# The second head's turned shares copied by ScalarE instead of VectorE, in a fused two-model kernel

## What is computed

```
p = softmax(mask(q @ k.T * scale + bias))     # 128 queries at a time, keys 0..(i+1)*128
out = p @ v
```

## Time and profile before

| | |
|---|---|
| median of 3 runs | 2183.3 us (2180.8 to 2186.79) |
| the profiled execution's own time | 2181.09 us |
| its span, first to last instruction | 2179.3 us |
| mean granted TensorE clock | 0.986 |
| busy: TensorE matmuls | 2073.2 us (95%) |
| busy: VectorE, ScalarE, GpSimd | 45%, 42%, 40% |

### The profile page before, as it was taken

The page is one execution under the profiler, slowest core; times in us unless marked ns, Lnnn a source line. Parts: engine busy times, 40 slices in busy tenths (PEclk is TensorE's granted clock), DMA queues, the critical chain, the costliest instruction groups (busy, mean ns, idle before and its releaser), DMA issues. The chain is left out here.

```text
span 2179.3 us, 28917 instructions
## 1 busy us (share of the span) xinstructions
PE 2073.2 (95%) x10248; PEld 1652.2 (76%) x10248; DVE 986.0 (45%) x1312; ACT 910.2 (42%) x1773; POOL 874.4 (40%) x648
## 2 busy tenths in 40 slices
PE   7999999999999978899999998989999999999997
PEld 5887688888887756688888886766667878888885
DVE  6454545312255677542312265666554544323134
ACT  4555443323343654442323355655554333223233
POOL 3232254444454221254444453542113545445454
PEclk9999999999999999999999999999999999999998
DMA  4212122222222110122222221221101222222222
GB/s 142 68 68 78 39 97 97 97 97 96 97 97 87 58 39 20 39 97 97 97 97 96 96 97 66 89 87 40 39 30 58 97 84 91 99 95 97 100 94 104
DMA packets 50613, 177.96 MB, mean 82 GB/s; under 512 B 5568, under 2 KB 5832, under 8 KB 50512
## 3 DMA queue, kind: packets, MB, share of 16 engines
q1 hardware_dynamic: 47536, 171.08, 22.6%
q10 hardware_dynamic: 2976, 5.48, 0.7%
HBM read 174.43 MB, written 2.12 MB: 81 GB/s over the span
## 5 line engine op out<-in xcount | busy, mean ns | idle before, releaser
L424 POOL TENSOR_TENSOR w_lo<-raw,w_hi 128x512 fp32r<-128x512 f32 x644 | 874.2, 1379 | 1285.1 <-ACT w_hi L1021 1285.1
L1021 ACT ACTIVATE w_hi<-raw 128x512 fp32r<-128x512 f32 x644 | 371.0, 624 | 849.1 <-PE gemm_banks L451 828.8
L449 PE MATMUL gemm_banks<-h_hi,w_hi 128*128 128x512 f32 x1512 | 613.7, 406 | 8.0 <-POOL w_lo L424 2.8
L451 PE MATMUL gemm_banks<-h_hi,w_lo 128*128 128x512 f32 x1512 | 592.7, 392 | 0.0
L450 PE MATMUL gemm_banks<-h_lo,w_hi 128*128 128x512 f32 x1512 | 592.1, 392 | 0.0
L449 PEld LDWEIGHTS gemm_banks<-h_hi,w_hi 128*128 128x128 f32 x1512 | 284.6, 188 | 92.4 <-issue 24.2
L449 PE MATMUL gemm_banks<-u_hi,w_hi 128*128 128x512 f32 x848 | 330.3, 390 | 4.2 <-POOL w_lo L424 2.9
L451 PEld LDWEIGHTS gemm_banks<-h_hi,w_lo 128*128 128x128 f32 x1512 | 284.2, 188 | 62.7
L450 PE MATMUL gemm_banks<-u_lo,w_hi 128*128 128x512 f32 x848 | 329.9, 389 | 0.0
L451 PE MATMUL gemm_banks<-u_hi,w_lo 128*128 128x512 f32 x848 | 329.9, 389 | 0.0
L450 PEld LDWEIGHTS gemm_banks<-h_lo,w_hi 128*128 128x128 f32 x1512 | 285.0, 188 | 56.6 <-issue 2.4
(11 more groups left out here) (308 smaller groups left out, 1980.2 us busy)
## 6 DMA issues: line engine op xcount, KB each, us to landing
raw<-slabs SPq DMA_DIRECT2D x322, 512.0 KB, 3.2
t_raw<-rel_rows ACTq DMA_DIRECT2D x4, 512.0 KB, 3.8
y_t<-x ACTq DMA_DIRECT2D x8, 256.0 KB, 2.1
x<-x_t SPq DMA_DIRECT2D x4, 256.0 KB, 6.7
x<-x_t ACTq DMA_DIRECT2D x4, 256.0 KB, 6.9
consts<-consts_packed SPq DMA_DIRECT2D x1, 516.5 KB, 8.7
cos<-pos SPq DMA_DIRECT2D x2, 256.0 KB, 10.1
params<-params_packed ACTq DMA_DIRECT2D x1, 211.5 KB, 4.3
```

The costliest lines, as they stand in the source:

```text
L424: pool.tensor_tensor(w_lo[:, j, part], raw[:, j, part], w_hi[:, j, part].bitcast(F32), ALU.subtract).then_inc(slab_split, 1)
L449: pe.matmul(out, high, rhs_hi, start=first, stop=False)
L451: return pe.matmul(out, low, rhs_hi, start=False, stop=last)
L1021: act.activation(w_hi[:, m % 2, part], raw[:, m % 2, part], ACT.Copy).then_inc(slab_hi, 1)
```

## The change

In the 80 steps that turn two heads' softmax shares (32 of the first block, 16 of the second, 32 of the third), VectorE's copy takes the first head alone, and a new ScalarE activation, `take_second`, copies the second head's. It stands in ScalarE's stream behind `weigh(s)` and the products' first half and ahead of `even(s)`. TensorE waits for both copies, by a second semaphore, ahead of every `bias_of` and `values`.

```
+            def take_second(n, w, need):
+                act.wait_ge(flipped, n + 1)
+                if need:
+                    act.wait_ge(valued, need)
+                act.activation(turned[:, 1, 0:w], SC[:, 2 * (n % 2) + 1, 0:w], ACT.Copy).then_inc(taken_b, 1)
...
                 if s < AB_STEPS:
                     weigh(s, (s % 4 + 1) * P)
                 products(*half(s, 0))
+                if s >= 1:
+                    take_second(s - 1, ((s - 1) % 4 + 1) * P, 2 * (s - 1))
                 if s < AB_STEPS:
                     even(s, (s % 4 + 1) * P, s + 1)
...
                 if s >= 2:
                     pe.wait_ge(taken, s - 1)
+                    pe.wait_ge(taken_b, second_takes(s - 1))
...
-                dve.tensor_copy(turned[:, :, 0:w], SC[:, 2 * b:2 * b + 2, 0:w]).then_inc(taken, 1)
+                dve.tensor_copy(turned[:, 0, 0:w], SC[:, 2 * b, 0:w]).then_inc(taken, 1)
```

More of the change, by code:

```diff
@@ L257, in e_valued, with second_takes @@
     return 128 + (s if s <= DIFF_STEPS else 2 * s - DIFF_STEPS)
+def second_takes(n):
+    first = AB_STEPS + STICK_STEPS
+    return min(n, AB_STEPS) + min(max(n - first, 0), CD_STEPS - STICK_STEPS) + max(n - E_BASE - DIFF_STEPS, 0)
 def build(nc, slabs, x_in, params_in, consts_in, pos1_in, pos2_in, rel_in, lam_in, y_out):
@@ L385, in build @@
         shared, evened, flipped = sem("shared"), sem("evened"), sem("flipped")
-        taken, valued = sem("taken"), sem("valued")
+        taken, taken_b, valued = sem("taken"), sem("taken_b"), sem("valued")
         qk_hi, qk_split = sem("qk_hi"), sem("qk_split")
@@ L576, in values @@
                 pe.wait_ge(taken, s + 1)
+                pe.wait_ge(taken_b, second_takes(s + 1))
                 if i == 0:
@@ L713, in cd_bias @@
                     pe.wait_ge(taken, AB_STEPS + s - 1)
+                    pe.wait_ge(taken_b, second_takes(AB_STEPS + s - 1))
                 mask = strict_r if p < 4 else chunk_r
@@ L752, in cd_values @@
                 pe.wait_ge(taken, AB_STEPS + s + 1)
+                pe.wait_ge(taken_b, second_takes(AB_STEPS + s + 1))
                 if i == 0:
@@ L895, in e_bias @@
                     pe.wait_ge(taken, E_BASE + s - 1)
+                    pe.wait_ge(taken_b, second_takes(E_BASE + s - 1))
                 for head in range(2):
@@ L936, in e_values @@
                 pe.wait_ge(taken, E_BASE + s + 1)
+                pe.wait_ge(taken_b, second_takes(E_BASE + s + 1))
                 if br == 0:
@@ L1306, in _ @@
                 cd_products(*cd_half(s, 0))
+                if s > STICK_STEPS:
+                    take_second(AB_STEPS + s - 1, ((s - 1) % 4 + 1) * P, 64 + 2 * (s - 1))
                 if STICK_STEPS <= s < CD_STEPS:
@@ L1411, in _ @@
                 e_half(2 * s)
+                if s > DIFF_STEPS:
+                    take_second(E_BASE + s - 1, e_step(s - 1)[3], e_valued(s - 1))
                 if s < DIFF_STEPS:
@@ L1847, in cd_take @@
                     dve.wait_ge(valued, 64 + 2 * s)
-                dve.tensor_copy(turned[:, :, 0:w], SC[:, 2 * b:2 * b + 2, 0:w]).then_inc(taken, 1)
+                if s < STICK_STEPS:
+                    last = dve.tensor_copy(turned[:, :, 0:w], SC[:, 2 * b:2 * b + 2, 0:w])
+                else:
+                    last = dve.tensor_copy(turned[:, 0, 0:w], SC[:, 2 * b, 0:w])
+                last.then_inc(taken, 1)
             def cd_shares(s):
```

## The result

The changed kernel takes 2189.2 us (median of 12 runs, 2186.62 to 2190.85), the kernel before 2183.6 us on the same chip (12 runs, 2180.8 to 2186.79). The ratio is 1.0023, 95% interval 1.0014 to 1.0032: about 5 us slower. That is slower beyond doubt, and inside the 0.3% that the prediction set as its limit of "no change". The profiled execution took 2189.12 us, span 2187.3, granted clock 0.984 (the mean share of 2.4 GHz that TensorE was given; its other level is 1.2 GHz). The prediction said 2193 us, with 2186 to 2201 as its range.

The account below looks back on a forecast made before the run. TensorE, its matmuls filling 95% of the span, was taken as the bound. Blocks of +0.9, +3.9 and +3.7 us make +8.6; with 1.2 for clock, 2181.1 becomes 2190.9, and 2.2 to the median gives 2193, range 2186 to 2201.

Parts of the forecast that it names:

- The bound and the order: TensorE's waits for the copy matter; ScalarE's in-order stream, with its copy behind both Exps, decides each of 80 steps.
- Price of the copy: ScalarE's copy out of PSUM was put at 0.27, 0.37, 0.48 and 0.58 us for the four widths.
- late and early steps: Late: Exps delay ScalarE's copy, +0.39 to +0.61 us in the first block; early: ScalarE is free, -7.0 us in 17 steps.
- TensorE's 0.05 us after a copy: Time TensorE needs between a copy's end and the next bias, read from a VectorE copy and used for ScalarE's.
- the sum: The three blocks' changes in waits, less what is absorbed: +0.9, +3.9 and +3.7, in all +8.6 us.
- What is absorbed: Delays given back: in the second block -1.7 at stalls and 0.86 at a full VectorE queue; 2.3 us behind the swap.
- the stalls: Second block: three times a +0.57 us delay precedes TensorE's 2.4 us stall for VectorE's rotated query, giving back 1.7 us.
- the swap: Third block: ScalarE's copy behind the swap delays the bias +3.9 us; 2.3 us come back, leaving +1.6.
- The clock: Added TensorE idling of 7.6 us would lower the granted clock: 2.5 us, of which half, 1.2 us, was charged.
- Hidden after all: Rival, 25 in 100: late copies delay only TensorE and work in hand absorbs half the sum, +4 us, 2187.
- Faster: Rival, 6 in 100: ScalarE's Exps are over when the flips end, so waits shrink by 13.2 us everywhere, 2170.
- Much slower: Rival, 9 in 100: nothing absorbed, copies 0.1 us dearer in 30 late steps, full clock loss: about +20 us, 2204.

Follow-up runs that it names:

- late_only: Against the kernel before, ScalarE copies the second head only in the 31 steps where its copy comes late; VectorE copies both elsewhere: 2197.17 us, ratio 1.0063.
- early_only: Against the kernel before, ScalarE copies the second head only in the 17 steps whose Exps end before the flips do: 2172.56 us, ratio 0.9944.
- e_only: Against the kernel before, ScalarE copies the second head only in the third block's 32 two-head steps: 2188.36 us, ratio 1.0019.
- copy_twice: Against the changed kernel, ScalarE makes each second copy twice before telling TensorE: 2215.87 us, ratio 1.0145 to the kernel before.
- second comparison: The changed kernel run once more, nothing changed: 2188.23 us beside 2184.79 of the kernel before, ratio 1.002.
- one-block kernels: Against the kernel before (2184.12 us), ScalarE copies the second head in one block only: first 2182.24, second 2182.47, third 2188.36 us.
- e_ahead: Against the changed kernel, the third block's ScalarE copy moved right behind the Exps: 2182.46 us, ratio 0.9998 to the kernel before.

## Why the prediction was right, and where its number was off

**The bound and the order.** Right. TensorE's wait for the copies is what the change moves, and the position in ScalarE's stream decides it: late_only and early_only, whose programs differ only in the list of steps, are 25 us apart.

**Price of the copy, late and early steps.** Right, to a few hundredths at the places written out: +0.41, +0.47, +0.57 and +0.68 for the first block's late steps against +0.39, +0.41, +0.60 and +0.61, and -0.53 and -0.54 for the early ones against -0.53. The first 26 steps are unchanged. What was too small is TensorE's 0.05 us after a copy. That is VectorE's: over 11 waits that end with a VectorE copy its median is 0.053 us, over 31 that end with ScalarE's it is 0.113 us. It adds 0.06 us to each of 31 late steps, 1.9 us. Before anything is absorbed the sum's terms make 13.5 us: late steps +20.5, early ones -7.0. Measured at these 48 waits are +22.3 and -7.2, so +15.1 us. The second block's late steps were the most too small, +10.4 against +8.1.

**What is absorbed.** Right for the stalls, wrong at the swap. In the second block the stalls for the rotated query shrank by what the bias ahead of them had lost; its copy waits grew by 8.5 us there and other gaps gave back 4.1, where the sum had 6.5 and 2.6. At the swap the sum let 2.3 us come back. The wait for the flips behind it did shrink, from 1.61 to 0.10 us, and the next late step waited 0.25 us less than before. Even so nothing had come back by then: the next bias comes 5.0 us later than before in the changed kernel's first trace and 4.4 in its second, 4.2 in e_only's, where the sum had 2.4. TensorE's work between the two biases ran at half the clock, which took what the shorter waits gave. These are TensorE's windows behind the swap, in the kernel before, the changed kernel and e_only:

```profile
1601.00:1608.00 7.00, 5.31 (x33) 3.29 (x32) 3.65 (x8) 5.35 (x12) 2.52 (x2) 1.00 0.21 76
```

```profile
1608.00:1615.00 7.00, 6.73 (x25) 4.55 (x26) 2.69 (x4) 2.48 (x7) 0.00 (x0) 0.51 0.24 76
```

```profile
1604.00:1611.00 7.00, 5.07 (x19) 3.24 (x20) 2.94 (x4) 3.51 (x9) 0.86 (x1) 0.51 0.24 75
```

All five traces with the long wait (4.8 us; 5.3 in copy_twice) have 1.2 GHz here. Of the other eight, with waits of 0.88 to 1.09 us, seven have the full clock, and early_only has a drop some 7 us later. So the swap cost 2 us more than its term.

**The whole.** I measured from load to load how much longer the three changed stretches are (steps 26 to 31, 48 to 63, 80 to 111), the clock included. The changed kernel's two traces against the two of the kernel before give 7.2 to 8.5 us in all four pairs; the sum had said 8.6, and 9.8 with its charge for the clock. By stretch it is +0.8 (forecast +0.9), +2.6 to +4.0 (+3.9) and +2.9 to +4.5 (+3.7). What differs between the pairs is all the rest, which the change leaves alone: +0.6 and +1.1 us against the first trace of the kernel before, -5.0 and -4.5 us against its second. So the third block's sum came out right partly by luck: the swap took 2 us more than its term, and the steps around it 2 us less, where the changed kernel's traces have 6.8 us at 1.2 GHz (steps 80 to 98) and those of the kernel before 10.2 and 13.7.

**The clock: the term in the wrong place.** The prediction charged 1.2 us all over, on the reading that TensorE's idling costs granted clock, and then added the 2.2 us by which the profiled execution lay below the median. At the swap there is such a charge, as shown. Over whole executions none shows: the changed kernel's mean granted clock was 0.9843 in 12 executions and 0.9846 in 9; that of the kernel before was 0.9832, 0.9843 and 0.9835 on three chips. Its first trace has 47.8 us at 1.2 GHz before the program's end, its second 64.9 us, and the changed kernel's two have 61.4 and 54.6 us. So the first profile of the kernel before was a favourable draw, at 0.986. With 8.6 us, no further charge for the clock and the median of before, the number would have been 2192.2; what is left, 3 us, lies outside the changed stretches, as far as these four traces tell.

**What stays open.** Taken over 144 executions, within each kernel and chip, 0.001 more clock went with 0.9 us less time. Corrected by that, early_only and late_only add up to +6.0 us, the whole is at +5.6 in its second comparison, and the one-block kernels add up to +3.6. Why one version is granted 0.986 and another 0.9825 was not settled by any run, and it is worth up to 3 us here. So the -12 us of early_only are -9 by that correction, where its waits said -7; that the waits give the larger part is shown, the rest only goes along with the clock.

**The rivals.** *Hidden after all* is refuted: late_only costs 13.8 us and copy_twice 32, where half of it hidden would have given far less. The time still came near that rival's 2187, for another reason. *Faster* holds where its condition holds, ScalarE's Exps over when the flips end: in 17 of 80 steps, and there to the amount forecast (-7.2 us for -7.0). The Trainium skill's advice (TensorEngine Tiling (Array Packing), PSUM Bottleneck) to use both engines for emptying PSUM agrees with early_only and disagrees with late_only: it holds where both engines are free at that moment. *Much slower* did not come; no copy was dearer by 0.1 us.

## What to carry to other kernels

Splitting a copy over two engines gains only at the steps where the second engine is idle when the data is ready; go through the stream step by step, and split there alone: 17 of 80 steps were worth 12 us, all 80 cost 5. Put a short piece of work that TensorE waits for directly behind the last instruction that must precede it, not behind a chain such as the swap (4.83 us of wait for a copy of 0.38, and half the clock after it). And before a difference of a few us is explained from a profile, or a profile used as a base, compare its granted clock with that of the kernel's other executions.

## What the runs showed of the hardware that was not expected

In the changed kernel's trace TensorE starts 0.113 us (median) after the end of a ScalarE copy that it waits for, and 0.053 us after a VectorE copy. A ScalarE instruction that follows another freely begins 0.10 us before that one ends, but 0.03 us behind its end when it waits for it by a semaphore (copy_twice). Behind a wait of 4.8 us, and not behind one of 0.9 us at the same place, TensorE ran at 1.2 GHz. Its time at 1.2 GHz before the program's end was 44.4 us in e_ahead's trace and 75.1 us in copy_twice's; the kernel before had 47.8 and 64.9 us in two executions.
